# The second weights of experts 1 to 29 issued by ScalarE behind its copies of y, the first weights alone on SyncE's queue

## The reference, cut to what matters

```
for e in range(32):
    z   = h2 @ w1[e] + b1[e]
    glu = minimum(z[..., 0::2], 7);  lin = clip(z[..., 1::2], -7, 7)
    act = glu * sigmoid(1.702 * glu) * (lin + 1)
    out = out + combine[..., e] * (act @ w2[e] + b2[e])
out = rms_norm(x + out)
```

## Time and profile before

| | us |
|---|---|
| median of 3 runs | 1089.05 (1087.67 to 1089.17) |
| the profiled execution, its own time | 1086.36 |
| its span | 1084.6 |
| PE busy | 1038.4 (96%) |
| DVE / ACT / POOL busy | 302.7 / 157.0 / 22.2 |
| DMA moved | 429.75 MB, mean 396 GB/s |

### The profile page before, as it was taken

One profiled execution on the slowest core, in us unless ns is written; L12 is line 12 of the kernel. 1 busy time (PEld: TensorE's weight loads), 2 busy tenths in 40 slices (PEclk: granted clock), 3 DMA queues, 4 the chain that ended last, 5 costly groups with the idle time before them and its releaser, 6 DMA issues.

```text
span 1084.6 us, 11586 instructions
## 1 busy us (share of the span) xinstructions
PE 1038.4 (96%) x4616; PEld 397.4 (37%) x4616; DVE 302.7 (28%) x705; ACT 157.0 (14%) x281; POOL 22.2 (2%) x29
## 2 busy tenths in 40 slices
PE   9999999999999999899999999898989898999996
PEld 7458454333333333233332323232323232333332
DVE  2455623322222223122221312221223222221221
ACT  1231333110101111101010111011111101011111
POOL 1212000000000000000000000000000000000000
PEclk9999999999999999999998999999999999899999
DMA  9886946999999999999999999999999999999995
GB/s 328 238 252 264 387 161 242 429 431 432 432 426 431 433 430 429 431 433 429 429 431 433 428 430 432 425 432 430 431 433 431 433 431 428 430 433 431 424 428 208
DMA packets 34343, 429.75 MB, mean 396 GB/s; under 512 B 5036, under 2 KB 6480, under 8 KB 16496
## 3 DMA queue, kind: packets, MB, share of 16 engines
q1 hardware_dynamic: 32400, 426.03, 93.2%
q10 hardware_dynamic: 1216, 1.70, 1.1%
q0 software_dynamic: 704, 1.71, 0.6%
HBM read 426.80 MB, written 2.62 MB: 396 GB/s over the span
## 4 chain that ended last, share of the span: by engine, by line
PE 67%; DMA 31%; DVE 1%; SPq 1%; issue 0%; ACT 0%; DVEq 0%
PE ps L1326 28%; DMA w1r<-w_mlp 22%; PE ps L1352 13%; DMA w2r<-w_mlp 6%; PE ps L1393 5%; PE ps L1076 4%; PE ps L1304 3%; PE ps L1064 3%; DMA w1r<-w_out 1%; PE ps L1123 1%; PE ps L1229 1%; PE ps L1366 1%; PE ps L1198 1%; DMA w1r<-w_in 1%; PE ps L1334 1%; PE ps L1312 1%
## 5 line engine op out<-in xcount | busy, mean ns | idle before, releaser
L1326 PE MATMUL ps<-w1r,arena 128*64 128x512 f32 x2048 | 487.7, 612 | 28.0 <-DMA w1r<-w_mlp 27.2
L1326 PEld LDWEIGHTS ps<-w1r,arena 128*64 128x64 f32 x2048 | 139.2, 139 | 295.7 <-issue 257.5
L1352 PE MATMUL ps<-w2r,arena 128*64 128x512 f32 x960 | 211.8, 593 | 4.5 <-DMA w2r<-w_mlp 4.5
L1352 PEld LDWEIGHTS ps<-w2r,arena 128*64 128x64 f32 x960 | 68.7, 137 | 142.8 <-issue 135.3
L950 DVE TENSOR_TENSOR acc<-ps,acc 128x512 f32<-128x512 f32 x56 | 36.1, 686 | 180.5 <-PE ps L1393 180.5
L942 DVE TENSOR_TENSOR arena<-arena 128x512 f32<-128x512 f32 x32 | 22.2, 692 | 157.5 <-ACT arena L571 157.4
L575 ACT ACTIVATE arena<-ps 128x512 f32<-128x512 f32 x32 | 19.1, 597 | 289.0 <-PE ps L1334 289.0
L914 DVE TENSOR_TENSOR arena<-ps,cols 128x512 f32<-128x512 f32 x32 | 22.1, 692 | 137.6 <-PE ps L1312 135.9
L1304 PE MATMUL ps<-h,arena 128*64 128x512 f32 x248 | 58.5, 592 | 0.0
L1393 PE MATMUL ps<-arena 128*128 128x512 f32 x112 | 55.5, 618 | 0.0
L580 ACT ACTIVATE arena<-ps 64x512 f32<-64x512 f32 x29 | 17.1, 591 | 263.8 <-PE ps L1352 263.8
(11 more groups left out here) (252 smaller groups left out, 575.4 us busy)
## 6 DMA issues: line engine op xcount, KB each, us to landing
w1r<-w_mlp SPq DMA_DIRECT2D x54, 4096.0 KB, 32.0
w2r<-w_mlp SPq DMA_DIRECT2D x60, 2048.0 KB, 18.9
w1r<-w_mlp SPq DMA_DIRECT2D x22, 2048.0 KB, 10.6
w1r<-w_in SPq DMA_DIRECT2D x7, 2048.0 KB, 17.3
w1r<-w_out SPq DMA_DIRECT2D x2, 2048.0 KB, 13.7
w1r<-w_mlp SPq DMA_DIRECT2D x3, 1024.0 KB, 7.3
rel_table<-arena ACTq DMA_DIRECT2D x1, 1536.0 KB
acc<-x SPq DMA_DIRECT2D x2, 512.0 KB, 4.6
```

The source lines that it names most:

```text
L1326: ins = mm(ps[64 * c:64 * c + 64, 2 * par + n, :], hgT[:, par, k % 4, 64 * (k // 4):64 * (k // 4) + 64], w1r[:, 8 * par + k, at:at + 512], ...
L1352: ins = mm(ps[at:at + 64, 4 + c, :], actT[:, k % 4, 64 * (k // 4):64 * (k // 4) + 64], w2r[:, k // 2, col:col + 512], start=(k == 0), stop ...
```

## The change

SyncE no longer issues w2 of experts 1 to 29. ScalarE issues both halves of w2(e) in step e, directly behind `take_y(e-1)`, so on its own DMA queue, and both when all of `down(e-1)` is done. SyncE's list for the sweep is now w1(2) to w1(31) in order and then `last_w2`. w2(0), w2(30) and w2(31) stay with SyncE. Buffers, counters and all other waits stay as they were.

```diff
@@ rest_of_sweep (SyncE)
-                def ahead(e, x, par):
-                    next_w2(base, e)
-                    next_half(base, x, par, 0)
-                    next_half(base, x, par, 1)
-
-                def between(e, x, par):
-                    next_half(base, x, par, 0)
-                    next_w2(base, e)
-                    next_half(base, x, par, 1)
...
                 next_w1(base, 3, 1)
-                ahead(1, 4, 0)
-                ahead(2, 5, 1)
-                ahead(3, 6, 0)
-                next_w2(base, 4)
-                with sp.Fori(3, 6) as m:
-                    between(2 * m - 1, 2 * m + 1, 1)
-                    between(2 * m, 2 * m + 2, 0)
-                with sp.Fori(6, NE // 2 - 1) as m:
-                    ahead(2 * m - 1, 2 * m + 1, 1)
-                    ahead(2 * m, 2 * m + 2, 0)
+                for x in (4, 5):
+                    next_half(base, x, x % 2, 0)
+                    next_half(base, x, x % 2, 1)
+                with sp.Fori(3, NE // 2 - 1) as m:
+                    for par in range(2):
+                        next_half(base, 2 * m + par, par, 0)
+                        next_half(base, 2 * m + par, par, 1)
+                for h in range(2):
+                    next_half(base, NE - 2, 0, h)
                 next_w1(base, NE - 1, 1)
-                next_w2(base, NE - 3)
                 last_w2(base)
@@ step (ScalarE)
                 if not (first and par == 0) and not last:
                     take_y(base, e - 1, 1 - par)
+                    for c in range(2):
+                        act.dma_start(w2r[:, 2 * c:2 * c + 2, :].rearrange("p a f -> p (a f)"), w2_v[e, c]).then_inc(w2_in[c], 16)
```

## The result

The changed kernel takes 1124.29 us (median of 3 runs, 1116.08 to 1130.55) against 1089.05 us: a ratio of 1.0331, 95% interval 1.0301 to 1.0361. It is 35.2 us slower. 1110 us was forecast, at most 1120. The direction was right, and so was the mechanism by which w2 comes late. The size was not: the sum left out the time in which the DMA engines themselves run dry.

What follows compares the result with a forecast made beforehand. DMA bytes at 430 GB/s were taken as the bound. Late w2(28) moved the end of step 29 from 1009.6 to 1033.3 us; plus 75.0 less 2.4 gave a 1105.9 us span, so 1110 us measured, range 1095 to 1120.

Steps and rivals of the forecast that it cites:

- What bounds the kernel, and that SP's long wait is no waste: Sweep: weight loads at 430 GB/s set the pace; SP's 601.7 us wait for `down` wastes nothing, its queue being full.
- Issue on ScalarE costs nothing: ACT's queue: 58 issues moved there hide in ACT's idle time before the sigmoid; otherwise they would cost 27 us.
- w2 later by 3.5 us costs no throughput: w2's first half is issued 3.5 us later, which costs no throughput against an engine with other bytes to move.
- Turns by packet, w2 gets a third: Two loaded queues alternate packets, 16.4 KB against 32.7 KB, so w2 takes up to 29.3 us and is late; chance 0.74.
- equal bytes: Rival: queues share by bytes, w2 nearly on time, only the order at the end costs 7.7 us, 1097 us; chance 0.12.
- some 2 us beyond its bytes: Any load takes some 2 us more than its bytes need, so w2 needs 31 us at one third.
- The lead of PE becomes unused w1, and 21.3 us at the end: SP fills w1's places early while PE waits for w2; the end of the span comes 21.3 us later.
- The engines stay busy, but with bytes that are not needed yet: While PE waits for w2 in `down`, the DMA engines never idle; the rate stays 430 GB/s.
- the place in the order: w2(28) lands with w1(31) partly moved, at the bytes of 1029.7 us, the middle of 1019.8 and 1039.5.
- worse: Rival: w2 gets less than a third, SP runs out of places, both queues idle in each step, over 1140 us; chance 0.05.
- the ends of the range: w2(28) landing at either end of w1(31)'s move makes the kernel 11.5 or 31.2 us slower.
- The signs that were named: Expected in the changed profile: PE's waits, q10's packets, w2's landing, sweep rate, last bytes; landing within 21 us would refute.

Runs made afterwards that it cites:

- e5: Kernel before, one queue, but both halves of w2 issued only when all of `down` is done: 1088.58 us, ratio 1.0001 to the kernel before.
- e6: Changed kernel, but ScalarE issues the first half of w2 when half of `down` is done, ahead of `take_y`: 1115.61 us, 27.0 over the kernel before.
- e4: Changed kernel, two queues, but SyncE holds back w1(7) to w1(30) with its former waits on `down`: 1307.60 us, 220.6 over the kernel before.
- e8: Changed kernel with each 4 MB half of w1 issued as four loads with packets of 8 KB: 1107.56 us, 18.9 over the kernel before.
- e1: Changed kernel with each 4 MB half of w1 issued as two loads with packets of 16 KB, like w2's: 1103.60 us, 16.6 over the kernel before.
- e3: Kernel before, all loads on SyncE's one queue, but w1(e+2) goes ahead of w2(e): 1097.52 us, 10.5 over the kernel before.
- e2: Kernel before, one queue, with each half of w1 as two loads with packets of 16 KB: 1092.12 us, 5.1 over the kernel before.
- e9: Kernel before, one queue and its order, with each half of w1 as four loads with packets of 8 KB: 1099.25 us, 10.8 over the kernel before.
- e10: Kernel before, one queue, with w1 ahead of w2 and w1 in packets of 16 KB: 1103.44 us, 15.0 over the kernel before.
- e7: Changed kernel with each half of w2 issued as two loads with packets of 8 KB, w1's staying at 32 KB: 1178.00 us, 89.4 over the kernel before.

## Why the prediction was right and wrong

**What bounds the kernel, and that SP's long wait is no waste: right.** e5 delays w2 further at no cost.

**Issue on ScalarE costs nothing: right as far as seen.** An issue mostly takes 0.34 us on ACT's queue (the step above), but the second of a pair can take up to 2.7 us, and the sigmoid behind it waits for that 18 times, 12.1 us in all (changed kernel, waits of ACT):

```profile
ACT arena L559 <- issue: 12.1, 18, 2.6
```

There is no such wait before. It stays hidden: the only wait of PE for ACT behind 200 us is one of 0.3 us, as before. No run shows why an issue takes that long now and then.

**w2 later by 3.5 us costs no throughput: right on one queue (e5), wrong on two.** Inside a loop that PE waits for it is worth 8 to 9 us (e6). The sentence held "against an engine that has other bytes to move", and the engines did not always have them.

**Turns by packet, w2 gets a third: right.** The earlier trace rows showed it with packets of 1.5 and 2 KB, e4 with 16 and 32 KB. The rival "equal bytes" fell; in e8, where w2 is in time, 8.1 us are left, near its 7.7. The "some 2 us beyond its bytes" of a load were nearer to 4 for a pair of halves: 23.5 us in e1 for 19.5 us of bytes.

**The lead of PE becomes unused w1, and 21.3 us at the end: right.** e3 shows the mechanism alone. In the changed kernel PE has 20 us more to do behind the last byte than before. From the end of step 29 (the start of the next line) to the end of the span it took 72.5 us, where the working had 75.0 - 2.4 = 72.6:

```profile
1049.98 0.60 PE L1257 MATMUL ps<-bias,sel_z 96*64 96x512 bf16 x4
```

**"The engines stay busy, but with bytes that are not needed yet": the step that failed.** The line above ends step 29 at 1049.98 us; the sum had 1033.3. The lines of the changed kernel that show why (timeline, and the issue of the second half of w2(28) with its time to landing):

```profile
1021.74 0.34 ACTq L598 DMA_DIRECT2D w2r<-w_mlp  x1
...
1043.11 7.04 PE L1342 MATMUL ps<-w2r,arena 128*64 128x512 f32 x32
```

```profile
w2r<-w_mlp ACTq DMA_DIRECT2D x1, 2048.0 KB, 23.8
```

w2(28) is there at 1021.74 + 23.8 = 1045.5 us. By then as many bytes have landed as the kernel before had at 1027.5 us, so the place in the order was guessed well (1029.7, 2.2 us off); but the same bytes came 18.0 us later. `down(28)` even ran without a wait, about 1 us behind the landing. The sum took 430 GB/s as given, and the sweep ran at 421; 820 x (1 - 421/430) is 17 us. These are the idle engines and slow starts of the section on the profile (8.8 and 9.6 us), which the runs on one queue and those on two with smaller packets of w1 do not have (at most 0.1 us idle in e1, e2, e3, e5, e8, e9 and e10).

The prediction had the cause in its hands, but kept it for the rival "worse", with a chance of 0.05 and on the condition that w2 gets less than a third. (e4 shows how long both queues can be empty: from the landing of w2 at 659.7 us to the next issue at 665.17 us, 5.5 us.) It should have asked in the main case when both queues run out at once. That is when one load is left under way and the next issue of either queue waits for PE, as at 397 us above. At a third this is rare, but not absent, and the ends of the range took in only where w2(28) lands among w1(31), not that the whole scale shifts.

One thing stays open: the lower clock behind the stalls lengthens the loop as well (5.81 us for half a `down`), and no run took it apart.

**The signs that were named.** Held: PE waits for w2 of 60.3 us (45 to 65), none for w1, the first in step 3, some 35 us at the end without DMA, 8352 packets more on q10 (58 x 128 of data and 58 x 16 small ones; 7400 was said). Failed: the rate (425 to 435 said), the last bytes (near 1070 us said, 1087 measured), and w2's landing, where 25 us were said and the median is 14.3 us. The second halves, which the working was about, take 23.1 us in the median and 32.1 at worst; the median of all was the wrong number to name.

## What to carry to other kernels

When two queues feed one engine's work, ask what share the transfer that is needed first gets, by the packets on either side, and how long its buffer's loop (issue, load at that share, use) may take; a single queue in the order of need gives the urgent load the whole rate. A long wait of the issuing engine is no waste while its queue is full, and letting the less urgent stream run ahead fills buffers with bytes that nobody waits for. Before a bandwidth is taken as given in a sum, look for the moment at which all queues run out because the next issue of each waits for the same engine.

## What was not expected of the hardware

- Packets of 16 KB instead of 32 KB for w1, on one queue, cost 5.1 us in a sweep of 870 us (428 GB/s), packets of 8 KB 10.8 us (424 GB/s), where 430 GB/s was the rate of the kernel before. A packet of 32 KB took 1217 ns in the mean, one of 16 KB 615 (before), one of 8 KB 314 (e9): the smaller ones take a little more per byte.
- A load that starts on idle engines starts slowly: at such starts of the changed kernel single packets of 32 KB took up to 2.3 us, where 1.21 is the median. So a gap costs about twice its idle time there (8.8 us idle, 9.6 us of slow packets).
- Where the transfer that PE waits for has the smaller packets, the time is uneven: three runs of the changed kernel lie 14.5 us apart and three of e7 14.9 us (1165.09 to 1180.02), against 1.5 us for three runs of the kernel before. e1, with equal packets, spread over 5.8 us, and e8, where w2 has the larger ones, over 3.2 us (four runs each).
